# Two heads of one token tile per attention step, and an output product whose first tile may lead by eight units

## The reference

```python
for i in range(4):                       # first block; kind = i % 3
    # kind 0: index scores, top 64 keys per query, attention over them (12 heads of 64)
    # kind 1: three dilated groups of 4 heads, combined by their log-sum-exp
    # kind 2: block attention, which for 256 tokens is causal attention
    mix = attention_of_kind(x @ w_in, positions)
    mo  = memory_attention(qm, mem_n @ w_mem_kv[i])          # 4 heads, 256 memory rows, no mask
    x = layer_norm(ALPHA * x + concat(mix, mo) @ w_out[i])   # LN1
    x = layer_norm(ALPHA * x + swiglu(x, w_gate_up[i], w_down[i]))   # LN2
for l in range(2):                       # second block
    u = rms_norm(x) @ w_in_2[l]
    oa = diff_attention(...)             # 4 heads, softmax(map 0) - lam * softmax(map 1)
    oa = rms_norm(oa, da_subln[l]) * (1 - lam_init)
    ob = mla_attention(...)              # 8 heads, K = 96, low-rank queries and keys
    oc = sliding_window_attention(...)   # 8 heads, sinks
    y = g0 * ((oa * silu(a_z)) @ w_br_a) + g1 * ((ob * silu(b_z)) @ w_br_b) + g2 * ((oc * silu(c_z)) @ w_br_c)
    x = x + rms_norm(y @ w_out[l])
    x = x + sigmoid(x @ w_ple_gate[l]) * (p[l] @ w_ple_proj[l])
```

## Time and profile before

| | us |
|---|---|
| median of 3 runs (lowest, highest) | 1952.76 (1952.08, 1953.87) |
| profiled execution, its own time | 1967.28 |
| its span, first to last instruction | 1965.3 |
| mean granted TensorE clock | 0.986 |
| PE busy | 1886.9 (96%) |
| DVE busy | 828.6 (42%) |
| ACT busy | 938.8 (48%) |
| POOL busy | 1520.2 (77%) |

### The profile page before, as it was taken

The page is one execution under the profiler, slowest core; times in us unless marked ns, Lnnn a source line. Parts: engine busy times, 40 slices in busy tenths (PEclk is TensorE's granted clock), DMA queues, the critical chain, the costliest instruction groups (busy, mean ns, idle before and its releaser), DMA issues.

```text
span 1965.3 us, 27351 instructions
## 1 busy us (share of the span) xinstructions
PE 1886.9 (96%) x9610; PEld 1543.3 (79%) x9610; DVE 828.6 (42%) x1913; ACT 938.8 (48%) x1473; POOL 1520.2 (77%) x1332
## 2 busy tenths in 40 slices
PE   6999999999999999999999999999899999999998
PEld 5777888777888877788787778877788877778876
DVE  7784110446211245411057731126736344556534
ACT  3455444354444346444434644444437644545742
POOL 6758989885897977697976789796677886767784
PEclk9999999999999999999999999999999999999999
DMA  8444656564666554465545456664545555554442
GB/s 267 124 145 142 202 150 235 172 193 117 197 191 210 156 174 158 151 187 184 202 130 157 153 171 189 198 204 126 167 147 147 171 168 172 163 164 143 143 164 97
DMA packets 184269, 330.54 MB, mean 168 GB/s; under 512 B 12188, under 2 KB 44488, under 8 KB 184136
## 3 DMA queue, kind: packets, MB, share of 16 engines
q1 hardware_dynamic: 176224, 323.21, 53.6%
q10 hardware_dynamic: 7912, 5.59, 0.9%
HBM read 325.35 MB, written 3.41 MB: 167 GB/s over the span
## 4 chain that ended last, share of the span: by engine, by line
PE 82%; DVE 8%; POOL 5%; DMA 2%; issue 2%; ACT 1%; ACTq 0%; DVEq 0%
PE acc L1391 24%; PE acc L1392 23%; PE acc L1398 21%; POOL w_lo L1171 5%; PE tps L1338 4%; PE acc L1413 3%; PE ops L1455 2%; PE acc L1394 2%; PE tps L1431 2%; DMA raw<-in_w_down 1%; DVE QT L1550 1%; PE ops L1350 1%; DVE U L1820 1%; PE acc L1362 1%; PE acc L1364 0%
## 5 line engine op out<-in xcount | busy, mean ns | idle before, releaser
L1171 POOL TENSOR_TENSOR w_lo<-raw,w_hi 128x512 fp32r<-128x512 f32 (+2 forms) x1244 | 1479.6, 1226 | 407.2 <-ACT w_hi L1199 406.3
L1199 ACT CAST w_hi<-raw 128x1024 fp32r<-128x1024 f32 (+2 forms) x624 | 615.4, 991 | 777.7 <-PE acc L1398 597.7
L1391 PE MATMUL acc<-w_hi,xT_hi 128*128 128x512 f32 (+1 forms) x1808 | 692.1, 386 | 13.1 <-issue 3.1
L1392 PE MATMUL acc<-w_lo,xT_hi 128*128 128x512 f32 (+1 forms) x1808 | 670.6, 374 | 0.0
L1398 PE MATMUL acc<-w_hi,xT_lo 128*128 128x512 f32 (+2 forms) x1744 | 508.3, 373 | 1.1 <-DVE xT_lo L1650 1.1
L1391 PEld LDWEIGHTS acc<-w_hi,xT_hi 128*128 128x128 f32 x1808 | 344.4, 190 | 87.7 <-issue 22.8
L1392 PEld LDWEIGHTS acc<-w_lo,xT_hi 128*128 128x128 f32 x1808 | 345.0, 191 | 52.8
L1398 PEld LDWEIGHTS acc<-w_hi,xT_lo 128*128 128x128 f32 x1744 | 319.9, 190 | 60.5 <-DVE xT_lo L1650 2.8
L1710 DVE TENSOR_TENSOR H<-G,acc 128x512 f32<-128x512 f32 (+1 forms) x48 | 30.9, 643 | 334.0 <-PE acc L1398 334.0
L1391 PE MATMUL acc<-w_hi,hT_hi 128*128 128x512 f32 x352 | 139.5, 396 | 5.1 <-POOL w_lo L1171 5.1
L1392 PE MATMUL acc<-w_lo,hT_hi 128*128 128x512 f32 x352 | 137.2, 390 | 0.0
(11 more groups left out here) (196 smaller groups left out, 2011.9 us busy)
## 6 DMA issues: line engine op xcount, KB each, us to landing
raw<-in_w_gate_up SPq DMA_DIRECT2D x160, 512.0 KB, 3.9
raw<-in_w_in SPq DMA_DIRECT2D x104, 512.0 KB, 3.7
raw<-in_w_down SPq DMA_DIRECT2D x88, 512.0 KB, 4.0
raw<-in_w_out SPq DMA_DIRECT2D x48, 512.0 KB, 3.7
raw<-in_w_in_a SPq DMA_DIRECT2D x32, 512.0 KB, 3.7
raw<-in_w_in_b SPq DMA_DIRECT2D x20, 512.0 KB, 3.9
raw<-in_w_mem_kv SPq DMA_DIRECT2D x16, 512.0 KB, 4.4
raw<-in_w_gate_up SPq DMA_DIRECT2D x32, 256.0 KB, 2.8
```

Of the source, the lines that this page charges most:

```text
L1171: ins = nc.gpsimd.tensor_tensor(w_lo[:, r, i, 0:ch.width], raw[:, r, i, 0:ch.width], w_hi[:, slot, i, 0:ch.width].bitcast(F32), ALU.subtract)
L1199: nc.scalar.copy(w_hi[:, u.u % SPLIT, 0:u.nk, 0:u.chunk.width], raw[:, u.u % RAW, 0:u.nk, 0:u.chunk.width]).then_inc(S["hi_ready"], 1)
L1391: nc.tensor.matmul(o, hi[:, tok], wh, start=first_k, stop=False)
L1392: ins = nc.tensor.matmul(o, hi[:, tok], wl, start=False, stop=False)
```

## The change

An attention step becomes two heads of one token tile. The 54 steps become 108: tile 0's steps come first, with one key tile each (128 keys instead of 384 columns for both tiles), then tile 1's, with two (256). Six steps' buffers (SETS) are in flight instead of three, the transposes of a step's two heads are one turn and one copy, and `PT` is two whole buffers that alternate. The work that feeds the steps goes tile by tile too: heads are transposed for one tile in fours (`tile_heads`), top_k, mask, `sub_scale` and the branches' transposes are per tile, and a step waits only for its own tile's (and for tile 1 also tile 0's keys) batches. Operations of one engine that covered both tiles become one for each: the scale on 128x8 becomes two on 128x4.

The output product of the first block gets `lead=True`: its tile-0 products wait only for tile 1's products eight units back (`n - SPLIT` instead of `n - LAG`) and have priority 0.4, so that they go beside tile 1's attention steps. The same eight hold for units shortly after a norm. Closing units get priority 0.7 + 0.1 t, ahead of the next stage's products.

```diff
@@ open_chunk
                     last = n - LAG
-                    if n < self.normed + SPLIT:
-                        last = min(last, self.normed - 1)
+                    if n < self.normed + SPLIT or lead:
+                        last = n - SPLIT
...
-                                    prio=1 + t, room=room)
+                                    prio=0.4 + 0.1 * t if lead else 0.7 + 0.1 * t if closing else 1 + t, room=room)
@@ attention
-            s.before3 = self.steps[-3] if s.s >= 3 else None
-            s.slot = s.s % 3
+            s.before2 = self.steps[-2] if s.s >= 2 else None
+            s.same_set = self.steps[-SETS] if s.s >= SETS else None
+            s.slot = s.s % SETS
...
-                s.turn[j] = self.task("PE", "turn", (s, j), 110 * blocks, "t_ready", [done], prio=0,
-                                      room=("tps", [(0,), (1,)]))
-                s.take[j] = self.task("DVE", "take_turn", (s, j), 160 + 1.03 * P * blocks, "t_taken",
-                                      [s.turn[j], b1.values if b1 is not None else None], prio=0)
-                s.turn[j].release = s.take[j]
...
+            blocks = s.turned * s.key_tiles
+            s.turn = self.task("PE", "turn", s, 110 * blocks, "t_ready", done, prio=0, room=("tps", [(0,), (1,)]))
+            s.take = self.task("DVE", "take_turn", s, 160 + 1.03 * P * blocks, "t_taken",
+                               [s.turn, b2.values if b2 is not None else None], prio=0)
@@ first block
-        out = lin(w["w_out"][l], 8, "mixed", spec[:1], banks=[[(0,)], [(1,)]], rows=MIXED)
-        out += lin(w["w_out"][l], 8, "mixed", spec[1:], hold=[[scored]] * T, banks=ANY, rows=MIXED, closing=True)
+        late = [(2,), (3,), (1,), (0,)]
+        out = lin(w["w_out"][l], 8, "mixed", spec[:1], hold=[[], [scored]], banks=[[(0,)], late], rows=MIXED, lead=True)
+        out += lin(w["w_out"][l], 8, "mixed", spec[1:], hold=[opened, [scored]], banks=[[(0,), (1,)], late], rows=MIXED, lead=True)
@@ second block, differential attention
-        combined = [s.outputs for s in steps]
-        sub = p.task("DVE", "stage", Stage("sub_scale", combined), 3200, None, combined)
-        gated = [p.stage(1500, "sub_gate", [sub, gained[t]], t=t, src=da, dst=da) for t in range(T)]
+        for t in range(T):
+            combined = [s.outputs for s in steps if s.t == t]
+            sub = p.task("DVE", "stage", Stage("sub_scale", combined, t=t), 3000, None, combined)
+            gated.append(p.stage(1500, "sub_gate", [sub, gained[t]], t=t, src=da, dst=da))
@@ scores
-                for t in range(T):
-                    c = tile_cols(s, t)
-                    for m in range(s.maps):
-                        (qt, base, n), (kt, kbase, _) = s.q[m], s.k[m]
-                        ins = nc.tensor.matmul(acc[:, k.slot[m], c], QT[base:base + n, qt, P * t:P * t + P],
-                                               KT[kbase:kbase + n, kt, 0:c.stop - c.start],
-                                               start=True, stop=True)
+                for m in range(s.maps):
+                    (qt, base, n), (kt, kbase, _) = s.q[m], s.k[m]
+                    ins = nc.tensor.matmul(score_columns(s)[:, m], QT[base:base + n, qt, tokens(s)],
+                                           KT[kbase:kbase + n, kt, 0:s.width], start=True, stop=True)
@@ sub_scale
-                    rms_columns(small[:, 5, 0:8], small[:, 7, :], RMS_EPS, small[:, 5, 8:16], small[:, 3, 8:16])
+                    c = slice(DA_H * t, DA_H * t + DA_H)
+                    rms_columns(small[:, 5, c], small[:, 7, 8 * t:8 * t + 8], RMS_EPS, small[:, 5, 8 + 4 * t:12 + 4 * t],
+                                small[:, 3, 8 + 4 * t:12 + 4 * t])
```

More of the change, by code:

```diff
@@ L511, in attention @@
             s.combine = self.task("DVE", "combine", s, cost, "combined",
-                                  [s.probs, b3.outputs if b3 is not None else None], prio=0)
-            for j in range(s.turns):
-                done = s.probs
-                if s.flavour == "differential":
-                    done = s.mixed = self.task("DVE", "mix_maps", s, 700, "maps_mixed", [s.combine], prio=0)
-                elif s.flipped:
+                                  [s.probs, s.same_set.outputs if s.same_set is not None else None], prio=0)
@@ L714, in plan @@
-        steps = [pair(6 + i, i, "MKV", MEMW + P * i, width=FULL, banks=[(2, 3), (0, 1)]) for i in range(2)] + steps
-        for s in steps:
-            if s.width != FULL:
-                s.fed = takes(vq)
-        for i in range(6 if kind != 1 else 0):
-            by_four = vq[:1] if kind == 0 else vq[-1:]
-            steps[2 + i].fed = takes(by_four if i < 4 else [c for c in vq if c not in by_four])
-        for s in steps:
-            if any(out[1] >= 4 for out in s.out):
-                s.clear = [x_used]
@@ L724, in plan @@
-        n = len(steps)
+        x_used = list(p.used["x"])
+        pairs_turned = [[[] for _ in range(3)] for _ in range(T)]
+        for t in range(T):
+            for i0, n, part in ((0, 2, 0), (2, 4, 1)):
+                for dst, col in (("QT", 0), ("KT", MIX)):
+                    first, stop = col + P * i0, col + P * (i0 + n)
+                    if kind == 1:
+                        fed = [chunks[c] for c in sorted({c // CHUNK for c in (first, stop - 1)})]
+                    else:
+                        fed = [halved[part][dst == "KT"]]
+                    done = p.tile_heads(src, list(range(first, stop, P)), P, dst, i0, t, takes(fed, [t]), clear_qk)
+                    for j in range(i0 // 2, (i0 + n) // 2):
+                        pairs_turned[t][j] += [b.take for b in done]
@@ L725, in plan @@
         if not l:
             steps[0].apart = [groups[-1].turn, lambdas]
[L727 to L733 removed]
+        p.attention(steps)
+        last_values, mem_values = steps[-1].values, steps[3].values
+        opened = []
@@ new lines, in outputs @@
+            def outputs(s):
+                if not s.flipped:
+                    heads_out(s)
+                    return
+                slot = s.values.slot[0]
+                dve.wait_ge(S["out_hi"], s.out_hi.n)
+                for half, tile, p0, p1 in s.out:
+                    hi, lo = act_tile("mixed", tile)
+                    ins = v.tensor_tensor(lo[p0:p1, tokens(s)], ops[p0:p1, slot, P * half:P * half + P],
+                                          hi[p0:p1, tokens(s)].bitcast(F32), ALU.subtract)
+                ins.then_inc(S["out_taken"], 1)
```

510 lines of the change are left out of this document (242 added, 268 removed).

## The result

The changed kernel takes 1973.89 us (median of 4 runs, 1973.21 to 1982.21) against 1952.48 us before (4 runs, 1952.08 to 1953.87): a ratio of 1.0118 (95% interval 1.0091 to 1.0146) by the comparison of the runs, 21.4 us by the medians. Forecast were 1947 us, with a range of 1930 to 1967. It was wrong in size and in sign, and lies beyond the slowest rival's 1967.

What follows compares the result with a forecast made beforehand. PE, busy 96% of the span, was taken as the bound, with waits costing idle time and then slow products. Terms +31 - 22 - 8 - 12 + 5 = -6 us, put on the median 1952.76, gave 1947 us, range 1930 to 1967.

Steps and rivals of the forecast that it cites:

- The runs: Score and value matmul groups on PE: 77 more runs at 0.40 us of edges each, +31 us (20 to 34).
- The norms: PE's idle time and slow clock at norms, covered by closing units going first: 22 us saved (12 to 24).
- The differential tail: DVE's scale and gate chain behind the last differential head, tile 0's part moved to the middle: 8 us saved.
- DVE and POOL in the tail: Rival: added small DVE operations each wait for a w_lo, logits come late, 8 us unsaved: 1955 us, chance 0.13.
- Heads by tile: Turns of projected heads, latents' first products and w_out's first units wait less for tile 1: 12 us saved (6 to 16).
- added waits: Ends of w_out, where tile 1's units stand alone, and splits held by w_hi's eight slots: +5 us (2 to 20).
- The runs decide: Rival: all 182 runs paid in full, waits return elsewhere, only 25 of 42 us saved: +14, 1967 us; chance 0.24.
- More is gained: Rival: edges beside turns cost half and norms, heads and tail give more: 1925 us, middle value 1935; chance 0.13.
- the "lead" rival: Rival: PE lacks split units beside attention, 2 us for each of four output products: +2, 1955 us; chance 0.08.
- The signs of being wrong: Mean granted clock not above 0.986, w_lo waits up over 5 us, or a run between products costing other than 0.40.
- The clock's sign: PE's mean granted clock: the prediction is wrong if it doesn't rise above 0.986.
- The base: The summed difference of -6 us, worked out on the profiled 1967.3 us, put on the median 1952.76: 1947 us.

Runs made afterwards that it cites:

- the pairs: Changed kernel, with an even step's values held until the next step's probabilities are turned, so two steps' values stand side by side: 1962.17 us, ratio 1.0053.
- the extra matmuls: Kernel before plus closing priority and lead of eight after a norm, with 96 unused matmuls added: 64 rows 1992.17 us, in fours 1969.82, 128 rows 1958.6.
- the rules alone: Kernel before with only closing units at priority 0.7 + 0.1 t and units after a norm leading by eight; attention unsplit: 1937.6 us, ratio 0.9923.
- second trace of before: Kernel before, unedited, run and profiled once more: 1954.15 us, ratio 1.0012; its profiled execution has a span of 1951.7 us.

## Why the prediction was wrong, step by step

**The runs (forecast +31): right in mechanism, near in size.** The split groups show 0.40 and 0.36, the pairs give 0.40 for each run by the medians, the extra matmuls 0.31 and 0.35, and PE's busy time allows at most some 29 us in all. To count the added runs from the two orders was right. The alternative in the range, that an edge to a turn costs half, isn't needed: where four turns and a score group of tile 1 stand together between products, in five places of the changed kernel's trace, both take 1.28 us, and alone 0.45 and 0.84. Called wrongly were the value runs: they aren't short in their rows, as the scores are, but in their columns (`128*64`), and the kernels with extra matmuls say nothing on them.

**The norms (forecast -22, low end -12): mis-sized.** Measured 15 with the rules alone, 13 in the changed kernel. The covers themselves do what was worked out: 20.1 us of waits go at the five places. But 4.2 come back where PE next waits for a norm of DVE (tmp, 2.6 us before, 6.9 in the kernel with the two rules). With the closing priority alone this wait stays at 2.6, though PE comes there as early, so it goes with the lead of eight after a norm. The forecast had no term for what that rule costs. That the two kernels' medians are equal all the same (1935.91 and 1937.6) stays open; the times of the first spread from 1931 to 1942.

**The differential tail (forecast -8): failed.** This is the first step that fell: nearly nothing was saved. PE's waits for gated heads and mixed probabilities, 8.5 + 4.2 = 12.7 us before, became 0.4 + 5.9 and 4.7 for the latents' bank, 11.0 us. I reasoned that half of the gate leaves the chain and tile 0's is done early. Before, PE waited for the gated heads; after, it waits for what is queued on DVE behind the scale. DVE in the first differential attention:

```profile
1404.39 1.23 DVE L1522 SCALAR_TENSOR_TENSOR small<-small 128x4 f32<-128x4 f32 x1
1405.65 0.17 DVE L1523 TENSOR_SCALAR small<-small 128x4 int32<-128x4 int32 x1
...
1407.24 1.25 DVE L1526 SCALAR_TENSOR_TENSOR small<-small 128x4 f32<-128x4 f32 x1
...
1411.15 0.16 DVE L1597 TENSOR_TENSOR U<-turned,acc 128x16 f32<-128x16 f32 x1
```

POOL in the same stretch, and PE:

```profile
1397.43 8.17 POOL L1202 TENSOR_TENSOR w_lo<-raw,w_hi 128x512 fp32r<-128x512 f32 x6 [0.83 <-ACT w_hi L1228]
1407.20 2.48 POOL L1202 TENSOR_TENSOR w_lo<-raw,w_hi 128x512 fp32r<-128x512 f32 x2 [1.60 <-ACT w_hi L1228]
```

```profile
1406.46 0.63 PE L1423 MATMUL acc<-w_hi,xT_lo 128*128 128x512 f32 x2
1411.37 0.58 PE L1387 MATMUL acc<-xT_hi,w_hi 128*128 128x256 f32 x1 [4.28 <-DVE U L1597]
```

PE stands from 1407.09 to 1411.37 for the latents' bank, whose copy waits in DVE's list behind tile 1's twelve small operations. In the second layer it is tile 0's scale, put in the middle, that delays the mixing of the probabilities (POOL, DVE, then PE):

```profile
1709.10 2.52 POOL L1202 TENSOR_TENSOR w_lo<-raw,w_hi 128x512 fp32r<-128x512 f32 x2 [1.14 <-ACT w_hi L1228]
```

```profile
1706.77 1.21 DVE L1525 SCALAR_TENSOR_TENSOR small<-small 128x4 f32<-128x4 f32 x1
...
1709.20 1.22 DVE L1526 SCALAR_TENSOR_TENSOR small<-small 128x4 f32<-128x4 f32 x1
...
1713.37 1.45 DVE L1955 SCALAR_TENSOR_TENSOR L<-L,recips 128x256 f32<-128x256 f32 x1
```

```profile
1714.88 0.69 PE L1452 MATMUL tps<-ident,L 128*128 128x128 f32 x2 [4.46 <-DVE L L1955]
```

That is in the main the rival "DVE and POOL in the tail", to which I gave 0.13. It had every added operation wait and the logits late; in fact three of twelve waited for most of a w_lo in the first stretch and five in the second, and late were the latents' copy and the mixing. The twelve took 5.6 and 7.8 us, near the 7 of the forecast's mean; what failed was that they would not stand in PE's way.

The rows also answer the rule of the Trainium skill ("SBUF — State Buffer", section "SBUF: two separate sides"). While POOL works, from 1404.39 to 1405.60 and from 1407.20 on, a small operation takes 1.23 or 1.25 us; while POOL waits for ACT, 1405.65 to 1407.20, each takes 0.16 or 0.17. Each that waits ends with POOL's instruction: the last of the six w_lo ends at 1405.60 (1397.43 + 8.17), and the operation at 1404.39 ends at 1405.62. The trace agrees with the rule for these operations with two SBUF inputs. What I called "borne out in part" was POOL's own idle time, not a weakness of the rule.

**Heads by tile (forecast -12) and added waits (forecast +5): the second step that failed.** Set against the kernel with the two rules, the ledger's waits are 5.4 us less in the two latent attentions and 4.3 less in the differential stages with the layers' starts; but they are 6.4 more in the two window stages, 4.3 more in layer 3, 1.5 in layer 2 and 0.5 in the first two. In all 3 more, where 15 less were forecast (-8 -12 +5). The two gains that I named did come in part: PE's turns of projected heads wait 2.6 us instead of 4.6, and its waits before products that end by "issue", among them the latents', fall from 5.9 to 1.2. They are paid back elsewhere. In the window attention a step of one tile has half the work and the same chain through DVE, POOL and ACT; that PE therefore gets to it before it is done is my reading of the rows, which no run tests by itself:

```profile
1518.97 0.44 PE L1467 MATMUL ops<-PT,U 128*64 128x128 f32 x4 [0.92 <-DVE PT L1937]
```

Before, copies of turned probabilities cost these values 0.9 us once; now 4.3 in six waits, four of them (2.5 us) in the two window stages and two in layer 3. In layer 3 the gate's second chunk waits for a bank that ACT hasn't read:

```profile
1136.52 0.61 PE L1423 MATMUL acc<-w_hi,xT_lo 128*128 128x512 f32 x2
1140.12 0.50 PE L1416 MATMUL acc<-w_hi,xT_hi 128*128 128x512 f32 x1 [2.98 <-ACT G L1258]
```

```profile
1137.11 1.05 ACT L1228 CAST w_hi<-raw 128x1024 fp32r<-128x1024 f32 x1 [1.13 <-DMA raw<-in_w_gate_up]
1138.17 1.28 ACT L1258 ACT_TABLE_LOAD   x1
1139.47 0.60 ACT L1258 ACTIVATE G<-acc 128x512 f32<-128x512 f32 x1
```

ACT has the activation in its list behind the split of a unit (1137.11) and a table load (1138.17). I expected the lead to do this through the ring of loads. Without the lead this wait is 0.7 us instead of 3.0, so it goes with the lead, but others grow (copies of turned probabilities in the stage from 1.8 to 2.6 us) and the kernel isn't faster. Through which path the lead does it stays open; it is some 2 us. One reading of the rows was wrong besides: of the four waits of 5.7 us for x_rows in the earlier trace rows two stand at ends of w_out, not three.

**The rivals.** "The runs decide" was the right rival, at 0.24: it names a loss from the point where less than 36 us are saved. Saved were 15 less 3 by the ledger. Its own price, 1967 us, was too low because it still allowed 25 saved. "More is gained" and the "lead" rival are refuted.

**The signs of being wrong.** None of the three that were named came: the mean granted clock is 0.992 and so above 0.986, waits for w_lo are 6.5 us against 6.0, and a run between products costs what it was said to. They watched the terms that were right, and none watched the waits on DVE. The clock's sign was worth little, since the second trace of before has 0.991 as well.

**The base.** I laid the difference of the sums on the median although the trace stood 15 us above it. The sum itself was made of local differences, so this did no harm by itself, but the changed kernel's trace (1971.2) against the first trace (1965.3) would have read as 6 us, and only the second trace gives the 19.5.

## What to carry to other kernels

Before a step is cut in two for finer overlap, count in the new order how many stretches of matmuls of 64 rows or 64 columns stand alone between full ones, and multiply by a price read from one of them: here 77 x 0.4 = 31 us, more than the idle time of all waits that the cut aimed at (8.3 + 4.2 + 4.6 + 2 x 1.8 = 20.7 us). A wait for an engine's chain doesn't go when the last link's size is halved; ask what stands behind the chain in that engine's list. And take such a change apart before keeping it: the line on the closing units' priority alone is 16 us faster than before (0.9919), attention by tile with the leading w_out costs 36.

## What the runs showed of the hardware that I hadn't expected

A float32 matmul of 64 rows and 128 columns alone between rounded products of 128 rows costs 0.57 us, one of 128 rows 0.22 us, and a run of four of 64 rows 1.34 us. A group of all 128 rows but 64 columns of the array pays an edge too, 0.36 us. A small VectorE operation with two SBUF inputs took 0.16 us beside an idle GpSimd and otherwise lasted until GpSimd's instruction ended, up to 1.25 us. The TENSOR_SCALAR, with a single SBUF input, took 0.17 us at 1405.65 with GpSimd idle and 1.22 us at 1705.51 with GpSimd busy. Two traces of one kernel can differ by 8.4 us in the first 65 us, for one wait of 8.6 instead of 2.2 us and the low clock with it.
